# Fewer products open two output tiles together; the others take one tile after the other

## What is computed

```python
x = x + hybrid_mixer(rmsnorm(x, g_mix[l]), w_in[l], g_group[l], sinks[l], w_out[l], rel_table)
x = x + memory_cross_attention(rmsnorm(x, g_cross[l]), rmsnorm(mem, g_mem[l]),
                               w_xq[l], w_xkv[l], w_xo[l])
x = x + squared_relu_mlp(rmsnorm(x, g_mlp[l]), w_up[l], w_down[l])
```

```python
h_lat = modulate(rmsnorm_2(x, norm1_g[l]), sh1, sc1)
h_ctx = modulate(rmsnorm_2(ctx, norm1_g[l]), csh1, csc1)
z_lat = h_lat @ w_in[l]
...
attn_lat = blocked_diff_attention(q_lat, k_all, v_all, lam)
out_lat = mixer_merge(z_lat, attn_lat, lam_init, ...)   # ends in m @ w_out[l]
x = x + g1 * out_lat
h2 = modulate(rmsnorm_2(x, norm2_g[l]), sh2, sc2)
x = x + g2 * conv_ffn(h2, ffn_up[l], ffn_conv_w[l], ffn_conv_b[l], ffn_down[l])
```

## Time and profile before

| | before |
|---|---|
| median of 3 runs | 3706.75 us (3704.3 to 3713.53) |
| profiled execution, its own time | 3712.06 us |
| its span in the trace | 3710.3 us |
| mean granted clock of TensorE | 0.97 |
| busy: PE, PEld | 95%, 79% |
| busy: DVE, ACT, POOL | 42%, 26%, 55% |
| read from HBM | 379.86 MB, 104 GB/s over the span |

### The profile page before, as it was taken

One profiled execution on the slowest core, in us unless ns is written; L12 is line 12 of the kernel. 1 busy time (PEld: TensorE's weight loads), 2 busy tenths in 40 slices (PEclk: granted clock), 3 DMA queues, 4 the chain that ended last, 5 costly groups with the idle time before them and its releaser, 6 DMA issues.

```text
span 3710.3 us, 47230 instructions
## 1 busy us (share of the span) xinstructions
PE 3543.2 (95%) x18826; PEld 2915.9 (79%) x18826; DVE 1575.3 (42%) x2738; ACT 966.5 (26%) x2038; POOL 2027.3 (55%) x1216
## 2 busy tenths in 40 slices
PE   7998988999999999899999999999999999999999
PEld 6876677877789988778777787888779777887887
DVE  7844541234863221474455313340472555214430
ACT  2235434133102111221344312220121354212210
POOL 4565363653559987644433465665545332555655
PEclk9999999978999999899999999999999999999999
DMA  7533122322765444332211232332322121232323
GB/s 284 202 128 98 62 89 89 100 85 85 229 214 151 145 131 125 116 106 86 63 57 46 74 94 82 92 95 90 111 73 87 52 61 42 91 91 86 97 83 105
DMA packets 109868, 389.26 MB, mean 105 GB/s; under 512 B 12057, under 2 KB 16537, under 8 KB 108242
## 3 DMA queue, kind: packets, MB, share of 16 engines
q1 hardware_dynamic: 89280, 315.10, 27.1%
q10 hardware_dynamic: 20370, 71.13, 5.5%
HBM read 379.86 MB, written 6.32 MB: 104 GB/s over the span
## 4 chain that ended last, share of the span: by engine, by line
PE 85%; DVE 8%; ACT 3%; issue 2%; POOL 1%; DMA 1%; ACTq 0%; DVEq 0%; SPq 0%
PE ps L362 20%; PE ps L364 20%; PE ps L363 20%; PE ps L1432 3%; PE ps L1444 2%; PE ps L1003 2%; PE ps L483 2%; PE ps L484 2%; PE ps L485 2%; PE ps L1412 1%; PE ps L1144 1%; PE ps L379 1%; PE ps L380 1%; PE ps L381 1%; DVE ada L1903 1%
## 5 line engine op out<-in xcount | busy, mean ns | idle before, releaser
L2487 POOL CAST whi<-raw 128x1024 fp32r<-128x1024 f32 (+1 forms) x606 | 619.3, 1022 | 1622.3 <-DMA raw<-in_w 1622.3
L2489 POOL TENSOR_TENSOR wlo<-raw,whi 128x1024 fp32r<-128x1024 f32 (+1 forms) x606 | 1421.0, 2345 | 48.5
L362 PE MATMUL ps<-hhi,whi 128*128 128x512 f32 x1928 | 775.2, 402 | 20.0 <-DVE q L1515 8.6
L364 PE MATMUL ps<-hhi,wlo 128*128 128x512 f32 x1928 | 762.1, 395 | 0.0
L363 PE MATMUL ps<-hlo,whi 128*128 128x512 f32 x1928 | 759.3, 394 | 0.0
L362 PEld LDWEIGHTS ps<-hhi,whi 128*128 128x128 f32 x1928 | 364.5, 189 | 108.7 <-DVE q L1515 9.4
L363 PEld LDWEIGHTS ps<-hlo,whi 128*128 128x128 f32 x1928 | 364.7, 189 | 86.0 <-issue 6.7
L364 PEld LDWEIGHTS ps<-hhi,wlo 128*128 128x128 f32 x1928 | 364.4, 189 | 79.5
L362 PE MATMUL ps<-chi,whi 128*128 128x256 f32 x816 | 240.4, 295 | 0.3 <-POOL wlo L2489 0.3
L363 PE MATMUL ps<-clo,whi 128*128 128x256 f32 x816 | 233.7, 286 | 0.0
L364 PE MATMUL ps<-chi,wlo 128*128 128x256 f32 x816 | 233.1, 286 | 0.0
(11 more groups left out here) (402 smaller groups left out, 6717.9 us busy)
## 6 DMA issues: line engine op xcount, KB each, us to landing
raw<-in_w SPq DMA_DIRECT2D x574, 512.0 KB, 3.7
ada<-in_ada ACTq DMA_DIRECT2D x96, 512.0 KB, 4.6
raw<-in_w SPq DMA_DIRECT2D x16, 384.0 KB, 3.3
att_toe<-toe_dram ACTq DMA_DIRECT2D x12, 256.0 KB, 3.3
raw<-in_w SPq DMA_DIRECT2D x16, 192.0 KB, 2.3
x<-in_x SPq DMA_DIRECT2D x4, 512.0 KB, 9.9
cond<-in_cc ACTq DMA_DIRECT2D x2, 1024.0 KB, 7.3
kc_dram<-kc ACTq DMA_DIRECT2D x2, 1024.0 KB, 5.0
```

Of the source, the lines that this page charges most:

```text
L362: nc.tensor.matmul(o, whi[:, buf, c], hi[:, k, 0:n], start=(k == 0), stop=False)
L364: mm = nc.tensor.matmul(o, wlo[:, buf, c], hi[:, k, 0:n], start=False, stop=(k == kt - 1))
L2487: nc.gpsimd.tensor_copy(whi[:, buf, 0:c], raw[:, buf, 0:c]).then_inc(slab_hi, 1)
L2489: nc.gpsimd.tensor_tensor(wlo[:, buf, 0:c], raw[:, buf, 0:c], whi[:, buf, 0:c].bitcast(F32), ALU.subtract).then_inc(slab_split, 1)
```

## The change

One line. `lead` stays 2 only where the product's name, less its last letter, is one of four and the stream is the 512 tokens:

```diff
-                self.lead = 2 if ready is not None and kt == BLOCKS else 1
+                self.lead = 2 if ready is not None and kt == BLOCKS and name[0:-1] in ("q", "f_up", "o", "in_q") and n == T else 1
```

## The result

| | before | after |
|---|---|---|
| median of 20 runs each | 3706.81 us | 3713.59 us |
| ratio of after to before, 95% interval | | 1.0020 (1.0010 to 1.0029) |
| profiled execution, its own time | 3712.06 us | 3715.05 us |
| its span | 3710.3 us | 3713.2 us |

The changed kernel takes 6.8 us more, 0.2%: 3715.2 had been forecast, and no change by the bound of 0.3%. The interval leaves out 1, so the loss is there, but it is small. One of the 20 runs before took 5869.9 us; the ratio leaves it out, and it hardly moves the median.

What follows compares the result with a forecast made beforehand. TensorE bounds the kernel, busy 95% of the span. Terms 4.1 + 2.0 + 2.0 - 0.8 - 1.0 + 0.3 = +6.6 us, plus 1.8 for one clock fall, give +8.4: 3715.2 us, range 3705 to 3722.

Steps and rivals of the forecast that it cites:

- no change by the bound of 0.3%: Whole kernel: the forecast +0.23% is less than the 0.3% (11.1 us) a measurement can tell; chance of no change 0.67.
- The three gated products: Mixer's output, memory keys, cross-attention query: late blocks leave the single form more matmuls to do; +4.1, +2.0 and +2.0 us.
- The clock: Holes between blocks idle TensorE and drop it to half clock; one fall taken, at the mixer's output, +1.8 us.
- the rival: Clock falls at all three gated products, each sparse first tile handing a slow clock on; +12.0 us, 3718.8 us, chance 0.18.
- The stretched subtraction: Mixer's output: POOL's split stretches VectorE's low halves of blocks 5 and 6; price +4.1 us with it, 3.0 without.
- The context's output: Output of the context's layer 0, tiles now apart around two cross-attention units: one unit made cheap, -1.0 us (-2.1 to +0.4).
- The context's keys: Context keys of layer 0: swapped steps give two TensorE waits, 0.76 and 0.71 us, time to end; -0.8 us (-1.5 to 0).
- The MLP: MLP up product: single form ends 4.8 us later, absorbed by 8.6 us of later waits; +0.3; not absorbed, chance 0.12.

Runs made afterwards that it cites:

- holes filled: The changed kernel with 6 and 11 idle matmuls ahead of blocks 5 and 6 of the mixer's output, tile 0; 3712.44 us, ratio to before 1.0018.
- the pair back at the three products: The changed kernel with the pair given back to the mixer's output, the memory's keys and the cross-attention's query; 3707.63 us, ratio to before 1.0000.
- the second profile of before: The kernel before run once more with no edit, for a second profile of the same program; one run, 3710.27 us.
- the mixer's output alone: The kernel before with one tile after the other only at the mixer's output; 3715.02 us, ratio to before 1.0020.

## Why the prediction was right, and where it was not

**The three gated products.** This step held, term by term: 4.1 forecast and 4.0 measured at the mixer's output (holes filled), 2.0 and 2.1 at the keys, 2.0 and 2.2 at the query. Counting what is left to do when the last late block arrives is enough to price the form where it stands. The sum also has no term for a stage behind that takes some of the loss back. That is open: in the four profiles with the single form at the query the cross-attention behind it is shorter by 5.9 us on average, against 1.2 in the six with the pair.

**The clock.** One fall was taken, at the mixer's output, at 1.8 us. It came there in every profile that has the single form at this product without filled holes (four of four), and cost 2.3. The keys had none in the changed kernel, but one in each of the three other profiles with the single form there, at about 1.5 us; the query had none in four. So it is one or two falls in a run, not three, and of the three kernels that have all three and leave the holes as they are, the changed one had one fall, the two others two. The MLP's up product, which the prediction gave no fall, ran its first tile at half clock in all five profiles with the single form and handed that on to the second, where the waits behind absorbed it. The rule of the Trainium skill, TensorE: Matmul & The Clock Gate, section What's actually happening, that activity releases the throttle, agrees with the filled holes: idle work that computes nothing kept the clock at 1.00 and the stage 2.3 us shorter. That every sparse first tile hands on a slow clock, the rival, is not borne out, for the query's never did; but the mixer's output, the MLP's up product and mostly the keys did.

**The stretched subtraction.** That POOL's split makes it, as the page SBUF — State Buffer of the Trainium skill (section Who interferes with whom) has it, was shown by moving the split: 2.09 us became 0.69. The prediction had block 6 come 2.3 us earlier without the stretch, which leaves most of its hole of 3.2 us in place; it came 2.5 us earlier (6.77 us behind the first matmul instead of 9.28), and a wait of 2.05 was left. What makes that wait the prediction did not say: 1.7 us of it are three steps of the context's branch in VectorE's queue. Only my expectation for the experiment, with waits under 0.5, put the whole hole down to the stretch.

**The context's output.** This step failed. The price of -1.0 came from the earlier trace rows, a unit of 2.81 us ahead of the pair against 1.84 behind it, read as the gain of a tile beside a unit. The two rows are the same unit at half and at full clock (0.50 and 1.00), and neither has a tile in it. The waits show no gain (6.3 us with this edit alone against 5.3 before), and the ratio none that can be told, so the term is 0, or a small cost. The 4 us by which the changed kernel's trace is shorter there are the clock, and go with the query's form, not with this one.

**The context's keys.** The two waits did shrink, and the starts come 0.5 to 0.8 us earlier. Behind that the profile of after has a fall of the clock at 254 us that the profile of before has not, behind the same wait of 1.21 us. The rows of before and of after:

```profile
255.01 0.33 PE L1132 MATMUL ps<-cst,att_p 128*128 128x128 f32 x1 [1.21 <-DVE att_p L1206]
```

```profile
254.24 0.48 PE L1132 MATMUL ps<-cst,att_p 128*128 128x128 f32 x1 [1.21 <-DVE att_p L1206]
```

That and a second one make the +3.3 there. It is no price of the change: with the pair back at the three products, where these swaps stand too, the starts at 300 us are within 0.1 of those at 240, while the second profile of before, without the swaps, has a fall at 256.

**The MLP.** Forecast +0.3, measured -0.6, and 0.6 to 1.0 less in each of the five profiles with this edit: the absorption held, even with the half clock that the sum did not count.

Put together from the steps that the experiments bear out: 4.0 + 2.3 + 2.1 + 2.2 - 0.7 - 0.6 = 9.3 us, and the medians say 6.8, with an interval of 3.7 to 10.8. The forecast of 8.4 and this sum are both in it. Two things are in neither: the fall at the keys that three of four profiles have, 1.5 us each, and the shorter cross-attention of the four profiles with the single form at the query, 4.6 us more than in those with the pair. With both, the estimate is 9.3 + 1.1 - 4.6 = 5.8 us, in the interval too. So the medians can't choose between these sums, and that the forecast came within 2 us of them is in part luck: the term that failed was small, and what was left out has both signs.

## What to carry to other kernels

Where the inputs of a product trickle in, price the form by what is left to do after the last late block, once for each form, at each place; places where everything is there early cost nothing that a run here shows, and a lag is free where the engine waits later for something else. Before taking the difference of two rows as the gain of an edit, look at the granted clock of both: two differences that looked like effects of one edit here (1 us in the prediction, 4 us in the comparison of the traces) were the same work at two clocks. And sort all profiles by one edit at a time: so it showed that the 4 us go with another product's form. To see which part of a loss is a wait and which is the clock, fill the wait with idle matmuls and look at the length again.

## What was not expected of the hardware

A stretch of 300 us in one execution had matmuls 2% further apart (216 against 220 in 50 us) at granted clock 1.00, with TensorE busy all the time; it came at that place in two of the ten profiles (the first of before, and that of the mixer's output alone) and made 5 us of the first one's time; the second profile of before has such a stretch at 1150 (317 matmuls against 328 in 50 us), and so have four of the other kernels' profiles (319 or 320 against 326). And behind the same wait, of 1.05 us (the keys), 1.21 or 1.98 us, the clock fell in one execution and held in another. So a difference of some us between two single profiles of this kernel means nothing before a second profile, or medians, confirm it.
